# Modulation vectors by multiply-and-sum on VectorE instead of small matmuls on TensorE, and more of the weight splitting on GpSimd, in a two-block transformer kernel

## The reference

```python
def modulation(cond, w, b):            # cond 1024, w 1024 x 6144, b 6144
    m = jax.nn.silu(cond) @ w + b
    return jnp.split(m, 6, axis=-1)

def adaln_norm(x, g, shift, scale):
    return rms_norm(x, g) * (1 + scale) + shift
# per layer: h = adaln_norm(x, norm1_g, mx[0], mx[1]); x = x + mx[2] * y(h)
#            h2 = adaln_norm(x, norm2_g, mx[3], mx[4]); x = x + mx[5] * sq_relu_mlp(h2)
```

## Time and profile before

| | |
|---|---|
| time, median of 3 runs | 2348.0 us (2345.93 to 2351.69) |
| time of the profiled execution | 2345.6 us |
| its span | 2343.8 us |
| TensorE busy | 2124.5 us, 91% of the span |
| DVE, ACT, POOL busy | 1146.2, 976.5, 680.0 us |
| mean granted clock of TensorE | 0.958 of full speed |
| weight blocks issued by SP | 536 of 512 KB |

### The profile page before, as it was taken

The page is one execution under the profiler, slowest core; times in us unless marked ns, Lnnn a source line. Parts: engine busy times, 40 slices in busy tenths (PEclk is TensorE's granted clock), DMA queues, the critical chain, the costliest instruction groups (busy, mean ns, idle before and its releaser), DMA issues.

```text
span 2343.8 us, 31162 instructions
## 1 busy us (share of the span) xinstructions
PE 2124.5 (91%) x12636; PEld 1797.7 (77%) x12636; DVE 1146.2 (49%) x1768; ACT 976.5 (42%) x1532; POOL 680.0 (29%) x313
## 2 busy tenths in 40 slices
PE   7998897899989995998899899999978788798999
PEld 6997864699956774786678688888766787678999
DVE  4555654556565758236476421021165845576420
ACT  5444333355455332332364342133254443364643
POOL 1100000000000232343014344444433545236887
PEclk9999998799999998999999899999989999899999
DMA  7954465445544441221002122222212223114554
GB/s 245 277 188 143 144 235 205 153 163 191 183 148 158 146 180 73 77 94 71 11 19 99 63 99 99 99 90 99 90 60 85 73 99 117 54 55 144 183 186 153
DMA packets 83310, 296.06 MB, mean 126 GB/s; under 512 B 9944, under 2 KB 12128, under 8 KB 83040
## 3 DMA queue, kind: packets, MB, share of 16 engines
q1 hardware_dynamic: 78336, 282.10, 34.4%
q0 software_dynamic: 3456, 10.55, 1.5%
q10 hardware_dynamic: 1376, 1.43, 0.2%
HBM read 292.97 MB, written 4.11 MB: 127 GB/s over the span
## 4 chain that ended last, share of the span: by engine, by line
PE 74%; DVE 15%; ACT 6%; DMA 2%; issue 1%; POOL 1%; ACTq 0%; DVEq 0%; SPq 0%; POOLq 0%
PE ps L447 20%; PE ps L445 19%; PE ps L442 19%; DMA wr<-wstream 2%; PE ps L720 2%; PE ps L969 1%; PE ps L929 1%; PE ps L946 1%; ACT wh L407 1%; PE ps L491 1%; PE ps L874 1%; PE ps L1358 1%; PE ps L876 1%; PE ps L879 1%; DVE tm L1171 1%
## 5 line engine op out<-in xcount | busy, mean ns | idle before, releaser
L423 POOL TENSOR_TENSOR wl<-wr,wh 128x1024 fp32r<-128x1024 f32 x258 | 626.5, 2434 | 866.3 <-ACT wh L407 849.0
L442 PE MATMUL ps<-HH,wh 128*128 128x256 f32 (+1 forms) x2336 | 770.1, 330 | 29.7 <-ACT HH L1143 12.3
L447 PE MATMUL ps<-HH,wl 128*128 128x256 f32 (+1 forms) x2336 | 760.0, 325 | 26.1 <-POOL wl L423 14.3
L445 PE MATMUL ps<-HL,wh 128*128 128x256 f32 (+1 forms) x2336 | 762.5, 326 | 5.2 <-DVE HL L1157 4.1
L407 ACT ACTIVATE wh<-wr 128x1024 fp32r<-128x1024 f32 x440 | 460.0, 1051 | 362.4 <-PE ps L447 287.6
L442 PEld LDWEIGHTS ps<-HH,wh 128*128 128x128 f32 x2336 | 456.7, 196 | 76.7 <-issue 45.4
L447 PEld LDWEIGHTS ps<-HH,wl 128*128 128x128 f32 x2336 | 455.6, 195 | 62.4 <-POOL wl L423 16.6
L445 PEld LDWEIGHTS ps<-HL,wh 128*128 128x128 f32 x2336 | 455.4, 195 | 51.2 <-DVE HL L1157 14.7
L423 DVE TENSOR_TENSOR wl<-wr,wh 128x1024 fp32r<-128x1024 f32 x182 | 221.3, 1226 | 179.1 <-ACT wh L407 177.0
L1500 POOL TENSOR_TENSOR D<-EB 128x512 f32<-128x512 f32 x24 | 35.0, 1457 | 704.2 <-DVE EB L1278 657.5
L447 PE MATMUL ps<-HIDH,wl 128*128 128x512 f32 (+1 forms) x512 | 174.4, 341 | 0.0
(11 more groups left out here) (268 smaller groups left out, 2811.9 us busy)
## 6 DMA issues: line engine op xcount, KB each, us to landing
wr<-wstream SPq DMA_DIRECT2D x536, 512.0 KB, 3.3
NAB<-naskew POOLq DMA_DIRECT2D x16, 128.0 KB, 11.3
dilskew<-lines POOLq DMA_DIRECT2D x1, 2048.0 KB, 19.8
DILB<-dilskew POOLq DMA_DIRECT2D x2, 1024.0 KB, 9.9
CT<-consts POOLq DMA_DIRECT2D x1, 1152.0 KB, 12.3
X<-xin ACTq DMA_DIRECT2D x4, 256.0 KB, 8.5
X<-xin POOLq DMA_DIRECT2D x1, 1024.0 KB, 9.0
yout<-X SPq DMA_DIRECT2D x8, 128.0 KB, 3.6
```

What stands on the lines that cost most here:

```text
L423: ins = e.tensor_tensor(self.WL[i % NSPL][:, :], self.WR[n % NRAW][:, :], self.WH[i % NSPL][:, :].bitcast(F32), ALU.subtract)
L442: e.matmul(out, wh, xh, start=i == 0, stop=False)
L445: e.matmul(out, wh, xl, start=False, stop=False)
L447: ins = e.matmul(out, wl, xh, start=False, stop=i == len(ks) - 1)
```

## The change

`pe_mod` goes, with the bank, the copies and the transposes. The weights of the modulation are sent transposed (`w_mod_t`): block `ch` holds 128 output rows of 1024 inputs, 48 blocks per layer as before. `silu(cond)` is loaded to all 128 partitions (`COND`, three times, 1 MB each, from ACT's queue), and DVE multiplies a raw block with it and sums along the row, once per condition (once only for the chunks from 16 on in layer 1), straight into `MOD`. The raw buffer of such a block is free when DVE has done this. `stream_mod` places the blocks in the stream and `next(mod)` the DVE work: layer 0's 21 chunks behind steps f = 1 to 21 of the first FFN, 5 behind the "qk" pairs, 22 behind the steps of the second FFN; layer 1's 48 behind the 32 MLP steps and the 2 x 8 output columns of layer 0. `mod_bank` joins the ring of auxiliary banks. Before "pool from", POOL makes the low halves of two split blocks in three (by the block's number) and DVE the third; behind it POOL makes all, as before. The bias loads move from POOL's queue to ACT's, spread over the FFN steps.

```diff
     def by_pool(self, n):
-        return self.old is not None and n > self.old.W.ahead(self.old.W.upto["pool from"])
+        W = self.old.W
+        return W.part(n) % 3 > 0 or n > W.ahead(W.upto["pool from"])
...
                 if W.kinds[n - NRAW]:
                     w.wait_ge(*self.low(n - NRAW))
                 else:
-                    w.wait_ge(*self.c("dense").at(("blk", n - NRAW)))
+                    w.wait_ge(*self.c("m_ttr").at(("blk", n - NRAW)))
...
+    def stream_mod(self, l, n=1):
+        for _ in range(n):
+            ch = sum(1 for k in self.chunks if k[0] == l)
+            if ch < 48:
+                self.chunks[l, ch] = self.W.tile(("w_mod_t", l), ch, [(0, 1024)], False)[0]
...
+    def act_cond_silu(self, e, w, z):
+        w.wait_ge(self.loads["cond"], 16 * (z + 1))
+        self.table(e, "silu")
+        e.activation(self.COND[z], self.COND[z], ACT.Silu).then_inc(*self.c("cond").mark(z))
+
+    def dve_mod(self, e, w, l, z, chunks):
+        for ch in chunks:
+            n = self.old.chunks[l, ch] if self.old else 0
+            conds = 1 if l and ch >= 16 else 2
+            w.wait_ge(*self.c("cond").at(z))
+            w.wait_ge(self.slot_sem[n % NRAW], 16 * (n // NRAW + 1))
+            block = self.WR[n % NRAW]
+            for c in range(conds):
...
+                ins = e.tensor_tensor_reduce(out=P, in0=src, in1=S, scale=1.0, scalar=0.0, op0=ALU.mult, op1=ALU.add,
+                                             accum_out=self.MOD[:, l, ch, c:c + 1])
+                last = [("blk", n if self.old else (l, ch))] if c == conds - 1 else []
+                ins.then_inc(*self.c("m_ttr").mark((l, ch, c), *last))
...
-    def pool_bias_loads(self, e, w):
+    def act_bias_loads(self, e, w, f):
...
         for f in self.pe_ffn(e, w, 1, "n1"):
             if f == 7:
                 self.pe_bias_line(e, w)
+            if f >= 1:
+                self.stream_mod(0)
...
         for f in self.dve_ffn(e, w, 1, []):
             if f == 7:
                 self.dve_bias_line(e, w)
+            if f >= 1:
+                next(mod)
...
             for f in range(nf * part, nf * part + nf):
...
-            if l == 0:
-                self.fill_mod(mods, 1, 4 if part == 0 else 30)
+                if l == 0:
+                    self.stream_mod(1)
```

More of the change, by code:

```diff
@@ L368, in __init__ @@
         self.set_now = None
+        self.chunks = {}
         self.made = {"hi": 0, "lo_dve": 0, "lo_pool": 0}
@@ L616, in act_pairs, with dve_pairs @@
                 self.act_square(e, w, key, j, dst(j).rearrange("p h t -> p (h t)"), [self.c("out_cp").at((key, j))])
-    def dve_pairs(self, e, w, key, ks, pairs, dst, squares, free):
+    def dve_pairs(self, e, w, key, ks, pairs, dst, squares, free, mod=iter(())):
         for j in range(pairs):
@@ L629, in dve_pairs @@
                 self.dve_square(e, w, key, j - 1, 512)
+            next(mod, None)
     def pe_resid(self, e, w, key):
@@ L704, in dve_ffn @@
         self.dve_pairs(e, w, ("down", n), range(22), 4, lambda j: self.Y[:, 2 * j:2 * j + 2, :], True, y_free)
[L708 to L736, removed]
-            yield
@@ L739, in dve_mod @@
[L739 to L761, removed]
@@ L763, in fill_mod, with act_cond @@
-    def fill_mod(self, mods, l, n=1):
-        for _ in range(n):
-            next(mods[l], None)
+    def stream_mod(self, l, n=1):
[3 more added lines that the diff above has]
+                self.chunks[l, ch] = self.W.tile(("w_mod_t", l), ch, [(0, 1024)], False)[0]
+    def act_cond(self, e, w, z, free):
+        for x in free:
+            w.wait_ge(*x)
+        S = self.COND[z]
+        src = bass.AP(self.d_cond.tensor, 0, [[0, 128]] + [list(x) for x in self.cond_shape(z)])
+        e.dma_start(S, src).then_inc(self.loads["cond"], 16)
@@ L801, in dve_setup @@
         e.tensor_scalar(LB[:, 4, :], LB[:, 0, :], -1.0, None, ALU.mult).then_inc(*v.mark("lb"))
-    def pool_bias_loads(self, e, w):
-        w.wait_ge(*self.c("dense").at(("fu", 1, 0)))
+    def act_bias_loads(self, e, w, f):
         L = self.loads
[L808 to L829, removed]
-            src = bass.AP(self.d_sk.tensor, 255 - 128 * a, [[511, 128], [65536, 8], [1, 256]])
-            e.dma_start(self.DILB[:, a], src).then_inc(L["dilbias"], 16)
@@ new lines, in act_bias_loads @@
+        if f == 5:
+            e.dma_start(self.X[:, :, 256:512], self.d_x[:, :, 256:512]).then_inc(L["xctx"], 16)
+        if f in (6, 8, 10, 12):
+            a, r = (f - 6) // 4, (f - 6) // 2 % 2
+            w.wait_ge(L["naskew"], 16)
+            for kr in range(4):
+                src = bass.AP(self.d_nk.tensor, (kr - 2 * a - r + 7) * 31 + 15, [[464, 64], [64 * 465, 8], [1, 64]])
+                dst = self.NAB[64 * r:64 * r + 64, a, :, kr * 64:kr * 64 + 64]
+                e.dma_start(dst, src).then_inc(L["nabias"], 16)
@@ new lines, in act_bias_loads @@
+        if f == 9:
+            w.wait_ge(*self.c("skew").at("line"))
+            e.dma_start(self.d_line, self.LNT[0:8, :]).then_inc(L["line"], 16)
+        if f == 11:
+            w.wait_ge(L["line"], 16)
+            wide = bass.AP(self.d_line.tensor, 0, [[512, 8], [0, 128], [1, 512]])
+            e.dma_start(self.d_sk, wide).then_inc(L["dilskew"], 16)
+        if f == 18:
+            w.wait_ge(L["dilskew"], 16)
+            for a in range(2):
+                src = bass.AP(self.d_sk.tensor, 255 - 128 * a, [[511, 128], [65536, 8], [1, 256]])
+                e.dma_start(self.DILB[:, a], src).then_inc(L["dilbias"], 16)
@@ L1953, in dve_add_out, with pe_ff @@
                 self.dve_square(e, w, key, d - 1, T)
+            next(mod, None)
     def hid(self, l):
         return (self.HIDH1, self.HIDL1) if l else (self.HIDH, self.HIDL)
-    def pe_ff(self, e, w, l, T, rhs, mods):
+    def pe_ff(self, e, w, l, T, rhs):
         nf = 32 if l else 16
@@ L2008, in dve_ff @@
                 self.tm.release(key, self.c("g_lo"), (l, f))
-            if l == 0:
-                self.fill_mod(mods, 1, 4 if part == 0 else 30)
-            self.dve_add_out(e, w, ("ff2", l, part), l, T, 40, (l, part) == (0, 1))
+                next(mod, None)
+            self.dve_add_out(e, w, ("ff2", l, part), l, T, 40, (l, part) == (0, 1), mod)
     def layer_keys(self, l):
@@ L2175, in dve @@
         L = self.loads
[L2176 removed]
+        mod = self.dve_mod(e, w, 0, 0, range(26))
         self.dve_setup(e, w)
@@ L2189, in dve @@
         self.dve_pairs(e, w, "qk", range(8), 8,
-                       lambda j: (self.QT if j < 4 else self.KT)[:, 2 * (j % 4):2 * (j % 4) + 2, :], False, down)
+                       lambda j: (self.QT if j < 4 else self.KT)[:, 2 * (j % 4):2 * (j % 4) + 2, :], False, down, mod)
         for h in range(2):
@@ L2331, in weight @@
         return w
+    if name[0] == "w_mod_t":
+        return inputs["w_mod_2"][name[1]].T
     return inputs[name[0]][name[1]]
@@ L2359, in pack_vecs @@
         put(name, columns(inputs[name]))
-    put("cc", np.stack([columns(inputs["c_2"]), columns(inputs["c_ctx_2"])], 2).reshape(128, 16))
     for name in ("q_norm_g_2", "k_norm_g_2"):
```

121 lines of the change are left out of this document (76 added, 45 removed), and 2 rows, old and new, of the table at.

## The result

The kernel after took 2733.9 us (median of 4 runs, 2728.7 to 2745.0), the kernel before 2348.3 beside it: ratio 1.165 (1.161 to 1.169, the 95% interval, as with every ratio below). The forecast was 2715, range 2580 to 2865. The profiled execution took 2728.7 us, with a span of 2726.9.

A forecast was written before the change was run, and what follows sets the result against it. TensorE, 91% busy, was taken to bound the kernel before; after it, a ring through the raw buffers. Costs of 410 us less gains of 40 gave +370 on 2345.6: 2715 us, range 2580 to 2865.

The forecast's parts named there:

- The ring: FFN steps: next weights wait for mod(f-1)'s buffer, mod(f) waits behind silu(f); 11.6 us per step with POOL's stops; likeliest, 0.62.
- Its terms: FFN step from R, VectorE's end of mod(f-1): second block landed R + 4.65, high half R + 5.75, mod(f) done R + 10.2.
- The multiply-and-sum: VectorE's modulation instruction, 128x1024: taken as 1.3 us, two per FFN step 2.6; bounds 1.23 and 2.46.
- The half-rate rival: Every modulation chunk: multiply-and-sum takes 2.46 us each, 152 us more, 2865 us in all; chance 0.13.
- POOL's stops: FFN steps: POOL's low halves hold up VectorE's two-input instructions, 1.4 us per step on average, 0 to 2.4.
- The clock: Rival: TensorE's clock falls in the gaps, up to 1 us more per step in 68 steps, 2780 us; chance 0.15.
- One sign: Profile after: TensorE's busy share near half in the slowed steps and as before elsewhere.
- The exclusion alone: Rival: only VectorE and POOL excluding each other bounds the FFN step, 7.0 us per step, 2350 us; chance 0.04.
- Ahead of the second FFN: Stretch from the norm's root to the second FFN's first step: gain of 12.0 us, from 22.1 to 10.1.
- Off: layer 0: Layer 0's recurrence: removing TensorE's modulation matmuls from 15 of 24 steps gains 12 us, range 0 to 30.
- Off: the output columns: Layer 0's output columns: 10.5 us of modulation and transfer just hidden behind 10.9 of TensorE; cost 0, up to 5.
- The loads: COND loads with ACT's silus, and bias loads queued in front of weight transfers: cost 12 us, nothing to 30.

The follow-up runs named there:

- experiment 4: Kernel after with VectorE's modulation one chunk ahead in layer 0's MLP alone, both FFNs as in the change: 2594.2 us, ratio 1.105 to the kernel before.
- experiment 1: Kernel after with all low halves before "pool from" made by VectorE again: 2698.5 us, ratio 1.150 to the kernel before.
- experiment 3: Kernel after with VectorE doing the chunk of step f+1 at the end of its step f, same instructions and stream: 2392.3 us, ratio 1.019 to the kernel before.
- experiment 2: Kernel after with a third multiply-and-sum per chunk, condition 0 a second time: 2858.9 us, ratio 1.218 to the kernel before.
- experiment 5: Kernel before with only the bias loads moved to ACT's queue: 2361.2 us, ratio 1.0071 to the kernel before.
- experiment 6: Kernel before with bias loads on ACT's queue and POOL making two of three low halves before "pool from": 2383.4 us, ratio 1.0148.
- version 7: Experiment 3 with all low halves before "pool from" made by VectorE: 2353.8 us, ratio 1.0037 to the kernel before.

## Why the prediction was right, point by point

Stages of the profiled executions, from first to last silu or relu or between them:

| stage | before | after | difference | predicted |
|---|---|---|---|---|
| first FFN, 21 steps | 123.4 | 248.1 | +124.7 | +114 |
| down projection and "qk" pairs | 136.5 | 159.8 | +23.3 | +17 |
| vr and units | 92.6 | 73.0 | -19.6 | -16 |
| units' end to second FFN | 82.0 | 64.5 | -17.5 | -12 |
| second FFN | 125.2 | 246.6 | +121.4 | +117 |
| to layer 0's first relu | 755.7 | 754.2 | -1.5 | -12 |
| MLP, first part | 81.6 | 163.4 | +81.8 | +84 |
| columns between | 95.1 | 98.2 | +3.1 | 0 |
| MLP, second part | 81.6 | 146.9 | +65.3 | +66 |
| all the rest | | | +2.1 | 0 |
| sum | 2343.8 | 2726.9 | +383.1 | +370 with 12 for the loads |

One stage with the same program differed by 2 to 4 us between single executions (first FFN 248.1 here and 252.2 in experiment 4; MLP, first part, 163.4 and 165.4 in experiment 1), so rows of that size say little.

- **The ring** is shown: experiment 3 takes 342 us away by the order alone, experiment 4 its MLP part, experiment 2 adds 1.35 us per chunk.
- **Its terms** hold: second block landed and its high half begun at R + 4.6 (4.65), silu at R + 5.6 (5.75), two multiply-and-sums 2.36 (2.6).
- **The multiply-and-sum** took 1.21 us with 0.07 for reading the sum; the second starts 1.14 after the first. The half-rate rival (the third in the prediction's list, which calls it the second) falls: with two float32 sources in SBUF and a sum it ran as fast as the low half on VectorE, 1.23. The rule that the prediction took from the Trainium skill (Vector Engine (DVE) Microarchitecture Reference, Points that are easy to get wrong) is stated for the scalar-tensor-tensor form. Whether it is wrong or doesn't cover this instruction, which the trace calls CUSTOM_DVE_ANT, no run here shows.
- **POOL's stops** were 1.4 by forecast. Experiment 1 took 0.49 and 0.69 us off the FFN steps. But there VectorE has both low halves of a step itself, so this is the net worth of the split, not the size of the stops. The stops are there in the rows: NHL took 1.59 us beside one low half of POOL and 2.64 beside two, so 1.2 and 2.2 more than its 0.42, where the prediction had 0.8 and 1.9. The step of 11.8 fits the forecast 11.6.
- **The clock** fell, to 0.79 to 0.85 in the four stretches where it had been 1.00 in the FFN. It cost little: no silu of the first FFN and no relu of the MLP had ACT idle for TensorE, so TensorE's pace was no part of the ring, and the MLP's steps were even 0.5 and 0.3 us shorter than forecast. One sign did not come: TensorE's busy share was to be near half there, and was 68% to 74%, since at the lower clock the same matmuls keep it busy longer (167.59 and 169.20 us in the FFNs; 124.17 in the second before).
- **The exclusion alone** falls: experiment 3 keeps it whole and runs at 8.0 and 7.6 us per step instead of 11.8 and 11.7. Its price of 7.0 per step is near what is left there once the ring is gone.
- **Ahead of the second FFN** the forecast of 12.0 held: from the end of the norm's root to the first silu it is 11.0 us (564.49 to 575.50) instead of 23.4 (441.73 to 465.1). The other 5 us of that row lie earlier in the stage.
- **Off: layer 0.** Gain 1.5 us, forecast 12. The gain was there, 11.1 in experiment 1 (755.7 to 744.6); POOL's split takes 9.6 of it back, which the prediction had costed at 0 elsewhere. On the kernel before the split costs 5 us in this stretch (experiments 5 and 6), and with the chunks one ahead 2.5 (experiment 3 against version 7), so it isn't the same in every order.
- **Off: the output columns.** +3.1 us instead of 0 between the MLP's parts; the third multiply-and-sum put 7.5 more on them (98.2 to 105.7 for 8 chunks), so they were not hidden but just at the edge. The 3.1 by itself is within what a stage varies; experiment 1 has 101.6 for the same work, experiment 4, one ahead, 95.5.
- **The loads**, 12 by forecast, have no row of their own; they lie in the first FFN. Their place was mostly the stated one. ACT stood behind its own issues only once there, 4.1 us. But the two longest turns of the ring, 15.1 and 14.7 us, are those in which a large load passes the weights, `dilskew` (2 MB, issued at 158.70) and the two of `DILB` (244.11); weight blocks took 7.6 us to land in them, 4.2 in the turns between. Against the usual three turns (11.4 on average) that is 7 us, with the 4.1 about 11. So most of the 11 us by which the first FFN exceeds its own term is the term of the loads. On the kernel before the same move costs about as much (1.0071, 17 us of 2348), but there by ACT's time of issue (experiment 5).

```profile
158.70 0.70 ACTq L833 DMA_DIRECT2D dilskew<-lines  x1
...
169.91 1.06 ACT L417 ACTIVATE wh<-wr 128x1024 fp32r<-128x1024 f32 x1 [10.80 <-DMA wr<-wstream]
```

The mis-sized terms point both ways. Too low: layer 0 by 10, down projection and "qk" pairs by 6, second FFN by 4, the columns by 3. Too high: units and the stretch ahead of the second FFN by 9 together, the MLP by 3. That they partly cancel is luck, and part of why the sum came within 13 us; the steps of the ring, which make up nearly all of it, were not luck.

## What to carry to other kernels

When a new user joins a ring of buffers, write down after which of its engine's instructions it gives the buffer back, and which transfer that blocks. If the engine reaches its next instruction of this kind only behind work that waits for that transfer, the transfer time enters every step, whatever the engines' busy shares. Then move the new user one step ahead in its engine's order before touching its cost: here the same instructions took 342 us less. And look at each stage anew: the same idea hid behind "qk" and "wo" pairs and built a fresh ring in the down projection.

## What had not been expected of the hardware

- DMA issues on ACT's queue cost ACT itself 0.35 to 1.27 us each (lines 812 to 818 of the kernel of experiment 6), 5.3 us for six. Four in a row behind a 2 MB load took 9.50 us (experiment 5) and, in experiment 3, 10.45.
- The multiply-and-sum stands in the trace as two instructions, the product with its sum (1.21) and the read of the accumulator (0.07 to 0.08), and the next product starts with the read. The one at 577.34 took 3.42 us, nearly three times the median. POOL's two low halves ran from 574.79 to 579.68, and it ended 1.08 us behind them, about its own length:

```profile
L756 DVE CUSTOM_DVE_ANT_0 PROD<-wr,COND x108: 1209/1214/3419, 577.3 to 2077.0; 128x1024 f32<-128x1024 f32 x108
```
